# Feed-forward down projections by seven block products, and weight sums made by adding transfers in memory from launch on

## The chip, the cores and the metric

The kernel runs on one core of a Trainium2 chip. The metric is device time in microseconds (us), the median of several runs. A core has TensorE (PE, matrix products into the eight banks of PSUM), VectorE (DVE), ScalarE (ACT), GpSimd (POOL) and SyncE (SP), each with an instruction stream of its own, and 16 DMA engines that carry the transfers which SP, ACT and POOL issue. Engines wait for each other by semaphores.

## The reference

Two layers of a hybrid encoder work on 640 rows (512 of a prompt, 8 x 16 of samples) of 1024 features, in float32. Of each layer only the end matters here:

```python
def finish_layer(x, a, b, ga, gb, w_a, w_b, w_o, g1, b1, w_up, w_down, g2, b2):
    mix = (ga * (a @ w_a) + gb * (b @ w_b)) @ w_o
    x = layer_norm(ALPHA * x + mix, g1, b1)
    h = jnp.square(jax.nn.relu(x @ w_up)) @ w_down
    return layer_norm(ALPHA * x + h, g2, b2)
```

`w_up` is 1024 x 4096 and `w_down` 4096 x 1024. Before it stand one input projection, a differential attention of eight heads (against a cache of 512 positions) and a sliding-window attention.

## The kernel before

**Products.** Each float32 operand is split into a high part (`w_hi`, `xt_hi`, `act_a[0]`) and the rest (`w_lo`, `xt_lo`, `act_a[1]`), and each product is three matmuls: high x high, high x low, low x high. ACT makes the high part of a weight chunk (`high`, line 1245, or by halves `part_highs`, line 1753), DVE subtracts it for the low part (`low`, line 2133, or `part_low`, line 2755).

**Weights.** SP loads `weights` chunk by chunk (128 partitions x 1024, 512 KB, line 557) into a ring of four slots `w_raw`, in the order of use. A slot is free again when its low part is made. Weights arrive well ahead of TensorE as a rule.

**Feed-forward stage.** It runs in four parts of 1024 hidden features. The up projection of a part takes its output tiles in pairs: four pairs (in part 0 two plain tile pairs, then two such pairs). A pair (`combined_pair`) is a 2 x 2 block product with seven products in place of eight: the blocks are the halves of the contraction and of the 640 rows. For it DVE makes four sums of weight blocks per pair (`weight_sums`, lines 2734 to 2745) in the slots of `w_raw`, and the sums of the activations (`t`) are made once per layer. A pair is 7 x 4 x 3 = 84 matmuls of 320 columns. ACT copies PSUM banks to seed further sums (`up_seed`, line 1784), applies relu (lines 1799, 1806) and squares (lines 1893, 1898), and DVE makes the low part of the square (line 2783).

The down projection of a part is two calls of `row_group` (line 719 and the two after it): output halves of 512 columns, eight contraction tiles and five tiles of 128 rows, 2 x 8 x 5 x 3 = 240 matmuls of 512 columns, without blocks. DVE adds each finished bank into `rows` (line 2592). Order of work: up part 0, down part 0, up part 1, down part 1 and so on, the same in both layers.

**Launch.** The first products (line 1070) start when the first pieces of `x_t` and of two weight chunks are in; SP issues the rest of `x_t` behind them (lines 557 to 569). `x_t` is used one contraction tile after another, twelve matmuls for each.

**Heads.** For each of the eight heads ACT issues two loads of old keys (`kc`, 1 MB each, line 1304) and one of old values (`vc`, 2 MB, line 1312), each as soon as the previous head is through with the buffer. POOL has no work at all after the constants.

The diff touches the functions of the feed-forward stage on PE (`combined_pair`, `row_group` and the loop over parts), ACT and DVE, SP's order of loads, POOL's program, and many semaphore names, which are merged to free numbers.

## Time and profile before

| | us |
|---|---|
| median of 3 runs | 2148.25 (2148.22 to 2148.42) |
| the profiled execution, first to last instruction | 2145.2 |
| around the span (median less span) | 3.05 |
| PE busy | 2134.6 |
| DVE busy | 1469.7 |
| ACT busy | 1182.0 |
| POOL busy | 0.2 |

A view by stages (the windows view) gives for a stretch of time what each engine was busy and with how many instructions, the granted clock of TensorE (1.00 is its upper level, 2.4 GHz) and how busy the 16 DMA engines were. A group of instructions by line gives their mean duration. Matmuls overlap, so that their mean duration is not the time from one to the next. The timeline gives each instruction's start, and in brackets how long its engine had been idle before it and for whom.

### The profile page before, as it was taken

What the parts mean: (1) busy time and instruction counts of PE and PEld (TensorE: products, weight loads), DVE (VectorE), ACT (ScalarE), POOL (GpSimd) and SP (SyncE); (2) the same over time, 40 slices, a digit from 0 to 9 for tenths busy, and PEclk for the clock granted to TensorE, in tenths of its full rate; (3) what the DMA queues carried; (4) which work ended last, traced back from release to release, by engine and by line L of the source; (5) the groups of instructions that cost most, each with busy time, mean ns of one, the idle gap of its engine ahead of it and who ended that gap; (6) DMA issues with size and microseconds to landing.
All of it is one profiled execution on the core that took longest, in us unless ns stands there. A gap on an engine that the chain in (4) does not pass through costs nothing.

```text
span 2145.2 us, 38346 instructions
## 1 busy us (share of the span) xinstructions
PE 2134.6 (100%) x15100; PEld 1950.9 (91%) x15100; DVE 1469.7 (69%) x2420; ACT 1182.0 (55%) x2513; POOL 0.2 (0%) x4
## 2 busy tenths in 40 slices
PE   9999999999999999999999999999999999999998
PEld 7998889999989898989889888899999898989897
DVE  6757778677879373636667577786769793646466
ACT  4457776686625362627234677766865262627261
POOL 0000000000000000000000000000000000000000
PEclk9999999999999999999999999999999999999999
DMA  5367562421341222212333765525113412212231
GB/s 190 103 250 256 210 235 89 160 98 51 108 162 41 98 86 72 89 69 89 108 110 103 276 249 202 203 93 179 60 60 108 152 60 79 89 69 91 78 108 69
DMA packets 68162, 268.19 MB, mean 125 GB/s; under 512 B 10984, under 2 KB 12648, under 8 KB 61296
## 3 DMA queue, kind: packets, MB, share of 16 engines
q1 hardware_dynamic: 43136, 152.75, 20.2%
q10 hardware_dynamic: 24848, 112.99, 14.8%
q8 instruction: 121, 1.98, 0.4%
q14 instruction: 57, 0.47, 0.1%
HBM read 236.35 MB, written 25.95 MB: 122 GB/s over the span
## 4 chain that ended last, share of the span: by engine, by line
PE 98%; ACT 1%; DVE 0%; DMA 0%; issue 0%; DVEq 0%; ACTq 0%
PE PS L719 10%; PE PS L721 10%; PE PS L720 10%; PE PS L649 9%; PE PS L651 9%; PE PS L650 9%; PE PS L617 9%; PE PS L619 9%; PE PS L618 9%; PE PS L847 2%; PE PS L872 2%; PE PS L810 1%; PE PS L760 1%; PE PS L861 1%; PE PS L792 1%; PE PS L990 1%
## 5 line engine op out<-in xcount | busy, mean ns | idle before, releaser
L2133 DVE TENSOR_TENSOR w_lo<-w_raw,w_hi 128x1024 fp32r<-128x1024 f32 x178 | 215.9, 1222 | 243.9 <-ACT w_hi L1245 235.1
L617 PE MATMUL PS<-xt_hi,w_hi 128*128 128x320 f32 x1184 | 382.2, 323 | 0.3
L619 PE MATMUL PS<-xt_hi,w_lo 128*128 128x320 f32 x1184 | 365.7, 309 | 0.0
L618 PE MATMUL PS<-xt_lo,w_hi 128*128 128x320 f32 x1184 | 365.4, 309 | 0.0
L1245 ACT ACTIVATE w_hi<-w_raw 128x1024 fp32r<-128x1024 f32 x178 | 186.6, 1058 | 303.9 <-PE PS L721 284.2
L719 PE MATMUL PS<-w_hi,act_a_hi 128*128 128x512 f32 x800 | 312.3, 390 | 0.0
L720 PE MATMUL PS<-w_lo,act_a_hi 128*128 128x512 f32 x800 | 311.4, 389 | 0.0
L721 PE MATMUL PS<-w_hi,act_a_lo 128*128 128x512 f32 x800 | 311.4, 389 | 0.0
L617 PEld LDWEIGHTS PS<-xt_hi,w_hi 128*128 128x128 f32 x1184 | 222.7, 188 | 5.6 <-issue 4.3
L618 PEld LDWEIGHTS PS<-xt_lo,w_hi 128*128 128x128 f32 x1184 | 223.0, 188 | 0.1
L619 PEld LDWEIGHTS PS<-xt_hi,w_lo 128*128 128x128 f32 x1184 | 222.3, 188 | 0.0
L1272 ACT ACTIVATE rope_s<-PS 32x320 f32<-32x320 f32 x352 | 150.7, 428 | 56.1 <-DVE z_all L2124 28.2
L721 PEld LDWEIGHTS PS<-w_hi,act_a_lo 128*128 128x128 f32 x800 | 150.2, 188 | 31.5
L719 PEld LDWEIGHTS PS<-w_hi,act_a_hi 128*128 128x128 f32 x800 | 150.2, 188 | 31.4 <-issue 0.5
L720 PEld LDWEIGHTS PS<-w_lo,act_a_hi 128*128 128x128 f32 x800 | 150.2, 188 | 30.4
L2755 DVE TENSOR_TENSOR part_lo<-w_raw,part_hi 128x512 fp32r<-128x512 f32 x144 | 98.0, 688 | 56.2 <-ACT part_hi L1753 54.0
L1753 ACT ACTIVATE w_hi<-w_raw 128x512 fp32r<-128x512 f32 x130 | 78.5, 623 | 61.5 <-PE PS L721 48.8
L1753 ACT ACTIVATE part_hi<-w_raw 128x512 fp32r<-128x512 f32 x144 | 88.3, 623 | 31.1 <-DVE w_raw L2741 29.1
L649 PE MATMUL PS<-t_hi,part_hi 128*128 128x320 f32 x328 | 101.4, 309 | 0.0
L650 PE MATMUL PS<-t_lo,part_hi 128*128 128x320 f32 x328 | 101.4, 309 | 0.0
L651 PE MATMUL PS<-t_hi,part_lo 128*128 128x320 f32 x328 | 101.4, 309 | 0.0
L1784 ACT ACTIVATE PS<-PS 128x320 f32<-128x320 f32 x144 | 60.9, 423 | 69.7 <-PE PS L651 69.5
(338 smaller groups left out, 4770.6 us busy)
## 6 DMA issues: line engine op xcount, KB each, us to landing
w_raw<-in_weights SPq DMA_DIRECT2D x274, 512.0 KB, 3.5
kc<-in_k_cache ACTq DMA_DIRECT2D x32, 1024.0 KB, 7.9
vc<-in_v_cache ACTq DMA_DIRECT2D x16, 2048.0 KB, 8.7
gates_kept<-a_t ACTq DMA_DIRECT2D x8, 640.0 KB, 6.9
k_out<-k_t ACTq DMA_DIRECT2D x16, 320.0 KB, 2.4
v_out<-rows ACTq DMA_DIRECT2D x2, 2560.0 KB, 16.8
mix_a<-a_t ACTq DMA_DIRECT2D x2, 2560.0 KB, 12.2
rope_c<-gates_kept ACTq DMA_DIRECT2D x10, 320.0 KB, 3.1
```

Source lines behind the costliest of these rows:

```text
L617: mm(out, wh, hi[:, k, c], start=(k == 0), stop=False)
L618: mm(out, wh, lo[:, k, c], start=False, stop=False)
L619: last = mm(out, wl, hi[:, k, c], start=False, stop=(k == KT - 1))
L649: mm(up_bank(x), wh, moving[0][:, k], start=first and k == 0, stop=False, skip_group_check=True)
L650: mm(up_bank(x), wh, moving[1][:, k], start=False, stop=False, skip_group_check=True)
L651: last = mm(up_bank(x), wl, moving[0][:, k], start=False, stop=(k == KH - 1), skip_group_check=True)
L719: mm(out, xh, wh, start=(k == 0), stop=False)
L720: mm(out, xh, wl, start=False, stop=False)
L721: last = mm(out, xl, wh, start=False, stop=(k == KT - 1))
L1245: fn(w_hi[slot][:], raw[:, j, :], ACT.Copy).then_inc(w_hi_made[s], 1)
L1753: fn(parts_of(part)[0][part_place(n, o)][:], part_source(part, n, o), ACT.Copy) .then_inc(part_hi_made if o < 5 else w_hi_made[o - 5], 1)
L2133: v.tensor_tensor(w_lo[slot][:], raw[:, raw_of(s, n)[0], :], w_hi[slot][:].bitcast(F32), ALU.subtract)\
```

## The change

The diff has 1565 lines; these parts carry it.

1. The down projections of parts 1 and 2 (`BLOCK_PARTS`), in both layers, become block products too (`block_down`). The row tiles 0 and 2 against 1 and 3, the even against the odd contraction tiles, and the two output halves make 2 x 2 blocks: seven products of two row tiles each. Row tile 4 is computed in the plain way alongside. The 2 x 4 contraction steps are cut into eight "operands", each a weight block or a sum of blocks, of 1 to 3 output banks. Parts 0 and 3 keep `row_group`.
2. The sums of the weight blocks, those for the up pairs and those for `block_down`, are made in memory. POOL issues, from launch on and in one queue, 12 jobs of 8 transfers each (4 copies, 4 adding transfers, each waited for by the next that reads it). The transfers are 1 MB each, and 0.5 MB in the two jobs of part 0. DVE's `weight_sums` remain for the gates and the branches only.
3. A chunk of the feed-forward stage is now a slot of a second ring (`load_ring`, `ring_high`, `ring_low`): an up pair has four chunks (seven blocks of 512 columns), a `block_down` sixteen of 1024. SP waits for the job's sums before the first chunk of each part.
4. Around a `block_down`, DVE makes sums of the squared activations (`act_sums`), ACT and DVE split them (`sum_high`, `sum_low`), ACT copies pairs of banks (`block_seed`), and DVE adds banks into `rows` (`block_take`).

```diff
+BLOCK_PARTS = (1, 2)
+PAIR_RING, BLOCK_RING = 4, 16
+RING_SLOTS = 4
+TAKES = 9
+JOB_TRANSFERS = 8
...
+        RING = (8, 7, 0, 1)
...
+                else:
+                    if n in sums_at:
+                        sp.wait_ge(sum_dma, 16 * JOB_TRANSFERS * (sums_at[n] + 1))
+                    load_ring(n, j)
...
+        @block.gpsimd
+        def _(pool):
...
+            def put(dst, src):
+                pool.dma_start(dst, src).then_inc(sum_dma, 16)
+
+            def add(dst, src):
+                pool.dma_start(dst, src, accum_op=ALU.add, max_dma_last_dim=8 * D).then_inc(sum_dma, 16)
...
+                put(s1, a21)
+                put(s3, a11)
+                pool.wait_ge(sum_dma, 16 * (before + 2))
+                add(s1, a22)
+                add(s3, a21)
+                pool.wait_ge(sum_dma, 16 * (before + 4))
+                put(s2, s1)
+                pool.wait_ge(sum_dma, 16 * (before + 5))
+                add(s2, a11)
+                pool.wait_ge(sum_dma, 16 * (before + 6))
+                put(s4, s2)
+                pool.wait_ge(sum_dma, 16 * (before + 7))
+                add(s4, a12)
+                pool.wait_ge(sum_dma, 16 * (before + 8))
...
+            for j, (l, kind, part) in enumerate(SUM_JOBS):
+                (up_sums_of if kind == "up" else down_sums_of)(l, part, JOB_TRANSFERS * j)
...
+                operand(0, [(2, tile(0, 0), lambda: pe.wait_ge(d_taken, TAKES * d)),
+                            (3, tile(0, 2), lambda: pe.wait_ge(up_taken, 2 * q + 1)),
+                            (4, tile(0, 4), lambda: pe.wait_ge(c11_taken, q + 1))], True, even_ready)
+                operand(1, [(6, sum_tile(1, 0), lambda: pe.wait_ge(p5_copied, q + 1)),
+                            (7, sum_tile(1, 1), lambda: pe.wait_ge(up_taken, 2 * q + 2))], True,
+                        lambda u: u % 2 == 0 and pe.wait_ge(s_lo_ready, 5 * d + 1 + u // 2))
+                operand(2, [(0, sum_tile(2, 0), seeds(1)), (1, sum_tile(2, 1), None)], False,
+                        lambda u: u == 0 and pe.wait_ge(s_lo_ready, 5 * d + 3))
+                operand(3, [(2, tile(1, 0), None), (3, tile(1, 2), None), (4, tile(1, 4), None)], False, odd_ready)
+                operand(4, [(0, sum_tile(3, 0), seeds(2)), (1, sum_tile(3, 1), None)], False,
+                        lambda u: u == 0 and pe.wait_ge(s_lo_ready, 5 * d + 4))
+                operand(5, [(5, tile(0, 4), lambda: pe.wait_ge(c21_taken, q + 1))], True, lambda u: None)
+                operand(6, [(6, sum_tile(4, 0), None), (7, sum_tile(4, 1), None), (5, tile(1, 4), None)], False,
+                        lambda u: u == 0 and pe.wait_ge(s_lo_ready, 5 * d + 5))
+                operand(7, [(2, tile(1, 1), seeds(3)), (3, tile(1, 3), None)], False, lambda u: None)
...
-                        row_group(nth(l, AT_FF) + 8 * part + 4 + 2 * v, l * GROUPS + 4 + 2 * part + v,
-                                  act_a[0], act_a[1],
+                    if part in BLOCK_PARTS:
+                        block_down(l, part)
```

**POOL at launch.** POOL's stream before ended with the constants; this is what stands after them now, the first job (`up_sums` of layer 0, part 0) and the first row of the second:

```order
L759 DMA up_sums<-in_up_blocks 16x8192 x2
L762 DMA up_sums<-in_up_blocks 64x2048 [waits sum_dma]
L762 DMA up_sums<-in_up_blocks 64x2048
L759 DMA up_sums<-up_sums 16x8192 [waits sum_dma]
L762 DMA up_sums<-in_up_blocks 64x2048 [waits sum_dma]
L759 DMA up_sums<-up_sums 16x8192 [waits sum_dma]
L762 DMA up_sums<-in_up_blocks 64x2048 [waits sum_dma]
L759 DMA up_sums<-in_up_blocks 16x16384 [waits sum_dma]
```

Line 759 is a copy, line 762 an adding transfer; nothing but the queue's own semaphore holds them back.

**ACT at the start of the down projection of part 1.** The last rows of the up pair and what follows, in the kernel after; `w_hi_71`, `_69`, `_55`, `_56` are the four ring slots:

```order
L2267 ACTIVATE act_a_hi<-rope_s 128x640 [waits c21_taken,relu_odd]
L2272 ACTIVATE rope_s<-rope_s 128x640 [waits pair_hi_made]
L2321 ACTIVATE act_a_hi<-act_a_full 128x2x2x128 [waits s_sums] x2
L1589 ACTIVATE w_hi_71<-w_raw 128x1024 [waits ring_done,raw_loaded2]
L2330 ACTIVATE PS<-PS 128x1024 [waits d_taken,ring_done]
L2321 ACTIVATE s_hi<-s_full 128x1024 [waits s_sums]
L1589 ACTIVATE w_hi_69<-w_raw 128x1024 [waits ring_done,raw_loaded3]
L1589 ACTIVATE w_hi_55<-w_raw 128x1024 [waits ring_done,raw_loaded0]
L1589 ACTIVATE w_hi_56<-w_raw 128x1024 [waits ring_done,raw_loaded1]
L2321 ACTIVATE s_hi<-s_full 128x1024 [waits ring_done,s_sums]
```

Between the splits of weight chunks (line 1589) now stand splits of activation sums (line 2321) and copies of two banks (line 2330).

**DVE at the same place**, in the kernel after:

```order
L3225 SCALAR_TENSOR_TENSOR xt_full<-s_full,rope_s 128x256 [waits s_sums]
L3232 TENSOR_TENSOR act_a_lo<-act_a_full,act_a_hi 128x2x2x128 [waits s_hi_made] x2
L2541 TENSOR_TENSOR w_lo_72<-w_raw,w_hi_71 128x1024 [waits ring_hi]
L3232 TENSOR_TENSOR s_lo<-s_full,s_hi 128x1024 [waits s_hi_made]
L2541 TENSOR_TENSOR w_lo_70<-w_raw,w_hi_69 128x1024 [waits ring_hi]
L3250 TENSOR_TENSOR rows<-rows,PS 128x2x512 [waits row_evacuated0,ring_done,d_taken,row_evacuated1,row_evacuated2,row_evacuated3,row_evacuated4]
L3250 TENSOR_TENSOR rows<-rows,PS 128x2x512 [waits ring_done]
L2541 TENSOR_TENSOR w_lo_57<-w_raw,w_hi_55 128x1024 [waits ring_hi]
```

The low parts of the next chunks stand behind two additions into `rows` (line 3250), which wait for the end of operand 1.

## Rows read from the trace of the kernel before

**Rows 1.** The page: busy time by engine, and the granted clock in 40 slices:
```profile
PE 2134.6 (100%) x15100; PEld 1950.9 (91%) x15100; DVE 1469.7 (69%) x2420; ACT 1182.0 (55%) x2513; POOL 0.2 (0%) x4
...
PEclk9999999999999999999999999999999999999999
```
**Rows 2.** Waits of PE, all of them: line, waited for, us, times, longest:
```profile
PE PS L1078 <- DVE mask_cols L2904: 1.5, 1, 1.5
PE PS L1070 <- DVE xt_lo L2917: 0.9, 1, 0.9
```
**Rows 3.** Windows: down 0, up 1, down 1 of layer 0, down 2 of layer 1:
```profile
704.10:758.50 54.40, 54.40 (x242) 45.04 (x241) 21.91 (x27) 12.97 (x17) 0.00 (x0) 1.00 0.21 73
758.50:807.80 49.30, 49.30 (x338) 49.28 (x337) 33.59 (x52) 34.40 (x68) 0.00 (x0) 1.00 0.28 97
807.80:862.20 54.40, 54.40 (x242) 45.04 (x241) 21.91 (x27) 12.98 (x17) 0.00 (x0) 1.00 0.19 68
...
1979.10:2033.50 54.40, 54.40 (x242) 45.06 (x241) 21.88 (x27) 13.01 (x17) 0.00 (x0) 1.00 0.19 68
```
**Rows 4.** Groups by line and shape, 807.8 to 862.2: count, busy us, mean ns:
```profile
L720 PE MATMUL PS<-w_lo,act_a_hi 128*128 128x512 f32 x80 | 31.1, 389 | 0.0
...
L2133 DVE TENSOR_TENSOR w_lo<-w_raw,w_hi 128x1024 fp32r<-128x1024 f32 x7 | 8.6, 1225 | 26.8 <-ACT w_hi L1245 26.8
L1245 ACT ACTIVATE w_hi<-w_raw 128x1024 fp32r<-128x1024 f32 x7 | 7.4, 1059 | 32.0 <-PE PS L721 32.0
L2592 DVE SCALAR_TENSOR_TENSOR rows<-rows,PS 128x512 f32<-128x512 f32 x9 | 6.1, 687 | 4.1 <-PE PS L721 4.1
```
**Rows 5.** Groups by line and shape, whole span: a read of two banks, a narrow sum:
```profile
L1290 ACT ACTIVATE xt_hi<-PS 128x1024 fp32r<-128x1024 f32 x12 | 12.3, 1023 | 17.1 <-PE PS L1029 17.1
...
L2777 DVE TENSOR_TENSOR rope_c<-PS,p 128x320 f32<-128x320 f32 x28 | 13.6, 487 | 6.4 <-PE PS L651 6.2
```
**Rows 6.** Timeline of DVE after 807.8: start, duration, idle before and for whom:
```profile
811.57 0.82 DVE L2783 TENSOR_TENSOR act_a_lo<-rope_s,act_a_hi 128x640 fp32r<-128x640 f32 x1 [0.17 <-ACT rope_s L1898]
```
**Rows 7.** Windows: launch, before the first head, the first head's loads, the heads:
```profile
0.00:14.00 14.00, 11.53 (x62) 8.95 (x63) 8.15 (x15) 8.99 (x16) 0.20 (x4) 1.00 0.88 319
53.60:115.00 61.40, 61.40 (x369) 57.75 (x368) 44.79 (x63) 29.62 (x52) 0.00 (x0) 1.00 0.30 102
114.00:128.00 14.00, 14.00 (x98) 13.55 (x100) 4.73 (x6) 6.53 (x11) 0.00 (x0) 1.00 0.91 341
127.00:345.00 218.00, 217.87 (x2153) 189.28 (x2152) 161.69 (x388) 157.41 (x402) 0.00 (x0) 1.00 0.60 220
```
**Rows 8.** Timelines at launch, of ACT, of DVE and of PE:
```profile
11.48 1.37 ACT L1968 ACTIVATE xt_hi<-x_t 128x640 fp32r<-128x640 f32 x2 [1.02 <-DMA x_t<-in_x_cols]
...
12.25 3.22 DVE L2922 TENSOR_TENSOR xt_lo<-x_t,xt_hi 128x640 fp32r<-128x640 f32 x4 [0.95 <-ACT xt_hi L1968]
...
13.04 0.31 PE L1072 MATMUL PS<-xt_hi,w_lo 128*128 128x320 f32 x1
13.19 0.36 PE L1070 MATMUL PS<-xt_hi,w_hi 128*128 128x320 f32 x1
```
**Rows 9.** Transfers issued from 313 to 324, memory to memory: size, us to landing:
```profile
swk_keep_out<-in_swa_k_keep SPq DMA_DIRECT2D x1, 896.0 KB, 8.3
swv_keep_out<-in_swa_v_keep SPq DMA_DIRECT2D x1, 896.0 KB, 9.6
```
**Rows 10.** Window around those two copies:
```profile
313.00:324.00 11.00, 11.00 (x85) 9.41 (x85) 7.49 (x17) 6.55 (x17) 0.00 (x0) 1.00 0.90 367
```
**Rows 11.** The first head's second load of keys: issue, landing of both, first use:
```profile
117.14 0.36 ACTq L1304 DMA_DIRECT2D kc<-in_k_cache  x1
...
DMA to landing us min/median/max: 5.0/6.6/8.1
...
L760 PE MATMUL PS<-kc,z_all x256: 592/592/617, 127.6 to 1388.9; 128*32 128x512 f32 x128
```
**Rows 12.** DMA issues of the page, the slowest small load at launch:
```profile
cos<-in_cos_t SPq DMA_DIRECT2D x1, 320.0 KB, 8.1
```

More of the change, by code:

```diff
@@ L1925, in combined_pair @@
-                if u > first:
                     up_square(l, part, u - 1, 1)
-                if not begun and not second:
-                    up_fifth(l, part, u)
-                if not last:
-                    part_highs(l, part, u + 1, (1,))
-                else:
-                    high(0, down, skipped=1)
-                if not begun and not second:
-                    up_seed(l, part, u, 1)
-                if not last and not begun:
-                    part_highs(l, part, u + 1, (2,))
+                if not begun:
+                    ff_fifth(l, part, u)
@@ new lines, in block_down, with lows, takes @@
+            def block_down(l, part):
+                g = ring_block(l, part)
+                def lows(first, end):
+                    for c in range(first, end):
+                        ring_low(g + c)
+                def takes(*which):
+                    for i in which:
+                        block_take(l, part, i)
+                sum_low(l, part, 0)
+                sum_low(l, part, 1)
+                lows(4, 5)
+                sum_low(l, part, 2)
+                lows(5, 6)
+                takes(0, 1)
+                lows(6, 8)
+                sum_low(l, part, 3)
+                lows(8, 11)
+                sum_low(l, part, 4)
+                takes(2, 3)
+                lows(11, 13)
+                lows(13, 14)
+                takes(4)
+                lows(14, 17)
+                takes(5, 6)
+                lows(17, 19)
+                takes(7, 8)
+                lows(19, 20)
@@ L2871, in combined_pair @@
                     up_low(l, part, u, 0)
-                    low(1, down)
+                    next_low(l, part, u, 3)
                     up_low(l, part, u, 1)
+                    if block:
+                        act_sums(l, part, u)
             def constants():
```

771 lines of the change are left out of this document (544 added, 227 removed).

## The prediction

> **What bounds the kernel now.** The page comes first: PE is busy for 2134.6 of 2145.2 us, DVE for 69 and ACT for 55 per cent [rows 1]. The view of PE's waits is nearly empty, with 2.4 us, both at launch [rows 2]. So every microsecond of matmuls taken away is one of the span, as long as the other engines and the loads keep their lead; and everything that is late at TensorE is lost in full. The granted clock is at the 2.4 GHz level in every slice, so no part of the time hangs on it [rows 1]. The windows then show what a down projection costs: 54.4 us with PE busy throughout, the same in all parts and in both layers [rows 3]. In it are 3 x 80 matmuls [rows 4]; their mean duration of 389 ns overlaps with the next one's, for 240 x 0.389 would be 93 us. What one is worth is 54.4 / 240 = 0.2267 us. The 242 matmuls in the window's row include two at its edges.
>
> **The change, part by part.** The sum is made against the profiled span of 2145.2 us. The median lies 3.05 us above it, and that is added at the end.
>
> Matmuls. Counting `block_down`: its eight operands have 3, 2, 2, 3, 2, 1, 3 and 2 output banks, 18 in all, each with 4 steps of 3 matmuls: 216 of 512 columns in place of 240. It is 24 x 0.2267 = 5.44 us less, and with two parts in two layers 4 x 5.44 = **21.8 us** less. The up pairs keep their 84 matmuls.
>
> Work of ACT and DVE in a block projection, which now lasts 49.0 us. ACT splits 16 chunks at 1.06 us [rows 4], copies two banks three times at 1.02 us, the nearest row for that width [rows 5], and splits the activation sums (two of 512 and three of 1024 columns, 4.4 us): 24.5 us. DVE has 16 low parts at 1.225 us (19.6), the low parts of the sums (5.1), and nine additions into `rows`, five of them 1024 wide at 1.23 us and four at 0.69 [rows 4], 8.9 us: 33.6 us. Both fit into 49 us; before it was 13 and 22 [rows 3]. In the up pairs DVE sheds four weight sums each, and ACT splits three chunks of 1024 and a half one in place of seven halves, so that ACT's 34.4 of 49.3 us [rows 3] do not grow. All that is work beside PE and costs nothing.
>
> Hand-overs in a block projection. Counted from its start, the operands end at 8.2, 13.6, 19.0, 27.2, 32.6, 35.4, 43.5 and 49.0 us. The tightest is the first. Operand 1 needs the low part of the first activation sum at 8.2. Before, DVE ended the last low part of the squares at 811.57 + 0.82 = 812.4, which is 4.6 us after the projection's start [rows 6]. Four sums of 256 columns follow, at most 0.49 us each by the nearest row [rows 5], and one split of 0.69: 7.2 us, a lead of 1.0 us. The next is chunk 6. Its low part stands on DVE behind two additions into `rows` that wait for the end of operand 1 at 13.6; with 2 x 1.23 and 1.23 us it is made at 17.3, and operand 3 wants it at 19.0. In the second half the leads are 3 us and more, but for the sum of operand 6, 26.9 against 35.4. At the way back into the up pairs the first product of the next part is ready, and the bank copy it needs at 52.5 is done at 51.2. I put **0** for all this, with bounds of 0 and 1 us at each of three places in four projections, 12 us. As each lead is computed from durations that hardly vary, I take the low end, and 0.5 us for what I haven't seen.
>
> Launch. Here the new queue meets the busiest stretch. The engines are at 0.88 in the first 14 us [rows 7], and PE lives from hand to mouth: ACT waits for `x_t` 4 and 5 until 11.48, DVE makes the low part of 4 by 13.05, and PE takes it at 13.19, a beat late [rows 8]. Each microsecond that these loads lose is PE's. POOL now issues two copies of 0.5 MB right away and then two adding transfers of 0.5 MB. The two copies of 0.9 MB at 313 took, with two weight chunks and others, 4.04 MB in 11 us at 0.90 [rows 10], 2.45 us of all engines per MB; so 1.05 MB costs 2.6 us. The adding transfers begin when the copies have landed, at about 9 to 11 us, and take a share until `x_t` 6 and 7 are in; I put 1.4 us for that. Sum **4.0 us**, with bounds of 0 (the copies start too late and yield) and 8 (both adding transfers, twice a copy's cost, go before the last of `x_t`: 2.6 + 5.2). The Trainium skill (DMA: Bandwidth & Descriptors, Issuing engines are not separate DMA queues) says that transfers issued from GpSimd run on the same 16 engines as the others and interleave. No row of this trace shows a transfer from POOL beside SP's; if POOL's had engines of their own, the term would be 0 and the sum 4 us lower.
>
> The first head. Its second load of keys is issued at 117.1 and lands after 8.1 at most, at 125.2; PE wants the keys from 127.6 on, the second half of them a microsecond later [rows 11]. The engines are at 0.91 around it [rows 7]. If the queue takes a third of them, landing takes 12 us and PE waits 0.7 us; with half of them 16 us and 4.7. I take **1.5 us**, bounds 0 and 5. In the later heads a buffer is asked for some 22 us ahead and lands within 10, and the engines are at 0.60 [rows 7], so a doubled landing still fits. In layer 1 the queue should be done by its first head.
>
> The queue itself. SP waits for a part's sums before it loads them. A job is six transfers one after another (two of these steps with two at once). A copy of 896 KB landed in 8.3 us, and the second, with the first in flight, in 9.6 [rows 9]; that is 9.5 us for 1024 KB alone and 11 us for two at once. So the copies of a job take 11 + 9.5 + 9.5 = 30 us. No row shows an adding transfer. Its low bound is a copy's time, 30 us for a job's four; its high one the slowest landing per byte of the page, 8.1 us for 320 KB [rows 12], 26 us for 1024 KB, 104 us for four. A job is between 60 and 134 us. I take twice a copy, because an addition reads two sources and the copies are the nearest row: 30 + 60 = 90 us. Layer 0 has 5.5 such jobs (part 0's is half), due before the up projection of part 3, which began at 704.1 + 3 x 54.4 + 2 x 49.3 = 965.9 [rows 3]; less the 10.9 us saved by then and some lead for SP's loads, at about 950 us. 5.5 x 90 = 495 us: hidden, up to 950 / 5.5 = 173 us a job. The Trainium skill (Collectives: The Full Stack, The bandwidth ceiling) says that a reduction runs at about half a copy's rate, for its two source reads; a job would be 90 us by it, and nothing here shows it.
>
> Sum: 2145.2 - 21.8 + 4.0 + 1.5 + 0.5 = 2129.4 us of span, with 3.05 around it **2132.5 us**, 0.7 per cent less.
>
> **The rivals.**
>
> *Slower: the queue is late.* If a 1 MB job takes longer than 173 us (adding transfers of (173 - 30) / 4 = 36 us each, nearly four times a copy), SP stands at the sums of layer 0's part 3, all loads behind it in its queue stand too, and PE with them. Each microsecond above costs 5.5. It crosses zero at 176 us; at 200 us the loss is 5.5 x 27 = 149 in layer 0 and the time about 2280. For it: adding transfers are unknown here, six steps are in series, the heads' loads take 0.60 of the engines [rows 7], and POOL has never had work here. Against: even the high bound of 134 us leaves a lead of 950 - 5.5 x 134 = 213 us. The Trainium skill (SBUF — State Buffer, SBUF: two separate sides) has a rule that would bring it about: GpSimd cannot write a transfer's descriptors while VectorE runs an operation in a two-port mode. DVE is busy for 0.69 of the span [rows 1], and if POOL could issue in the rest only, the six steps of a job would be held up by some operations of 1 us each, 6 to 12 us a job, far from the 83 that are missing; so the chance of this rival is not raised by it.
>
> *No change: the leads are eaten.* Every hand-over of the blocks that misses costs PE. If the three places of a projection miss by 1.5 us each on top of their leads, it loses 4.5 of its 5.4 us, four of them 18 us, and the time is 2132.5 + 18 = 2150. For it: ACT and DVE serve three chains in one order there (chunks, activation sums, banks), and one that is late makes the others late. Against: the leads counted above, and engines for the loads that are 0.19 busy before [rows 3]. Contention alone would have to cost 17 us more than I count, over twice what the two high bounds (8 and 5) leave.
>
> *Much faster: the matmuls are worth their duration.* 96 x 0.389 = 37 us would give 2117. Only the mean duration speaks for it [rows 4], the windows speak against it [rows 3].
>
> **How the numbers follow.** The forecast (2126 to 2143.9) has 0.77. The queue that is late has 0.10, all of it slower. The eaten leads have 0.10, of which 0.09 lie within 0.2 per cent of 2148.25 (2143.95 to 2152.55, about what a measurement of this kernel can tell from no change) and 0.01 above. The price by duration and the like have 0.03. So faster 0.80, same 0.09, slower 0.11. The low end is 2126.0: the full 21.8 us with no loss at all is 2126.5. The high end is 2143.5: launch 8, head 5, and 2 of hand-overs give 2138.5, and 5 us are put on for several missed leads. Outside lie some 0.2.
>
> **What would show it.** PE should have 15100 - 96 = 15004 matmuls, a block projection should last 49.0 us with PE busy throughout, and PE's waits should stay empty but for launch and the first head. The first product with `x_t` 4 should start at about 17 us, not 13.2. POOL's transfers of a job should take 60 to 135 us in all and end for layer 0 by 740. Wrong would be: a wait of SP for the sums, PE idle between operands, or loads of keys that land after 12 us in later heads too.

## The result and the profile after

The changed kernel takes **2186.32 us** (median of 4 runs, 2183.24 to 2193.83) against 2148.32 beside it on the same chip: a ratio of **1.0183**, with an interval of 1.0165 to 1.0201. The prediction was 2132.5 with a range of 2126.0 to 2143.5. It is wrong in size and in sign, by 54 us. The profiled execution took 2187.98 us, its span 2186.2. (In one run further down, **e3_no_queue**, one of ten executions went at a granted clock of 0.654 and took 2981.4 us; the ratio there leaves it out.)

The page's busy row answers to [rows 1]. PE has 96 matmuls fewer, as counted, and yet stands at 97 per cent instead of 100:

```profile
PE 2129.3 (97%) x15004; PEld 1939.3 (89%) x15004; DVE 1469.5 (67%) x2336; ACT 1232.6 (56%) x2493; POOL 65.4 (3%) x100
```
The page's row of the clock still has a 9 in every slice; a slice is 55 us wide. The windows further down show what that hides.

The view of PE's waits, two rows before [rows 2], now has twelve, of which the eight costliest stand here (line, waited for, us, times, longest):

```profile
PE PS L911 <- ACT PS L2154: 15.5, 20, 0.9
PE PS L822 <- ACT rope_s L1622: 9.3, 1, 9.3
PE PS L1394 <- DVE xt_lo L3405: 7.0, 3, 4.8
PE PS L1116 <- ACT a_t L1729: 3.2, 1, 3.2
PE PS L1084 <- DMA kc<-in_k_cache: 2.9, 2, 1.5
PE PS L1043 <- DVE rows L3000: 2.6, 1, 2.6
PE PS L1043 <- DVE w_lo L2534: 2.5, 1, 2.5
PE PS L981 <- issue: 1.6, 4, 0.4
```
They fall into two kinds. The first row is 20 short waits in the up pairs, ten in each layer and hardly different from each other, which points to the program's own order. All others but the small issue gaps are single events of 1 to 9 us: at launch, at the first keys, at the gates, and in the output projection. Together the twelve are 48.9 us.

Windows show what stands beside them (length, PE, PEld, DVE, ACT, POOL busy, granted clock, DMA share, GB/s): at launch, behind the first keys, and around the wait at 461:

```profile
20.00:30.00 10.00, 8.81 (x45) 8.81 (x46) 8.00 (x15) 4.74 (x8) 1.22 (x1) 0.70 1.04 401
...
140.00:150.00 10.00, 8.68 (x75) 6.13 (x68) 2.47 (x5) 4.41 (x11) 0.00 (x0) 0.83 1.04 341
...
450.00:460.00 10.00, 1.55 (x13) 1.30 (x12) 0.00 (x0) 4.09 (x8) 0.52 (x1) 0.80 1.13 262
460.00:470.00 10.00, 9.14 (x46) 9.18 (x47) 4.70 (x9) 6.62 (x13) 0.37 (x1) 0.69 0.95 387
```
The DMA engines are full in each of them, where launch was at 0.88 and the heads at 0.60 before [rows 7]; and the granted clock falls behind PE's longer waits, to 0.69 from 460 to 470. So a wait costs more than its own length: around 461 PE waits for 1.2 and 9.3 us and loses 13.4. Its timeline has the longer wait, and products of 0.47 us behind it that take 0.31 at the clock's upper level. Eighteen of them start 0.27 us apart in place of 0.147:

```profile
460.86 0.61 PE L822 MATMUL PS<-xt_hi,w_hi 128*128 128x320 f32 x1 [9.31 <-ACT rope_s L1622]
461.26 0.47 PE L823 MATMUL PS<-xt_lo,w_hi 128*128 128x320 f32 x1
```

If the matmuls of both kernels are put side by side by their order, the lag of the changed kernel reads: +10.2 us at 30, +14.9 after the first head, +19.6 before the gates, +33.5 behind them, +39.9 at the feed-forward stage of layer 0, and +41.0 at the end. In this sum are 20.5 us that the block projections gave back (5.1 each, below). So 61 us were lost, against 6 in the prediction. (The median of the kernel before, run again beside the experiments, was between 2147.28 and 2148.40, so that medians of different runs can be compared to about 1 us.)

### The profile page after: what moved, and what is told of

Same layout as the page of the kernel before. It is cut to its first block, busy times and chain, and to the rows that moved or that the text cites. A ratio compares the mean times of both kernels' runs of the same rounds, so it can differ in the third digit from the quotient of the medians.

```text
span 2186.2 us, 38210 instructions
## 1 busy us (share of the span) xinstructions
PE 2129.3 (97%) x15004; PEld 1939.3 (89%) x15004; DVE 1469.5 (67%) x2336; ACT 1232.6 (56%) x2493; POOL 65.4 (3%) x100
## 3 DMA queue, kind: packets, MB, share of 16 engines
q0 software_dynamic: 7936, 92.28, 16.5%
## 4 chain that ended last, share of the span: by engine, by line
PE 86%; ACT 5%; issue 3%; DMA 3%; DVE 2%; SPq 0%; ACTq 0%; DVEq 0%
PE PS L822 9%; PE PS L824 8%; PE PS L823 8%; PE PS L1043 6%; PE PS L1045 6%; PE PS L1044 6%; PE PS L855 3%; PE PS L856 3%; PE PS L857 3%; PE PS L911 3%; PE PS L913 3%; PE PS L912 3%; PE PS L981 3%; PE PS L982 3%; PE PS L983 3%
## 5 line engine op out<-in xcount | busy, mean ns | idle before, releaser
L824 PE MATMUL PS<-xt_hi,w_lo 128*128 128x320 f32 x1184 | 367.2, 310 | 0.0
L823 PE MATMUL PS<-xt_lo,w_hi 128*128 128x320 f32 x1184 | 367.1, 310 | 0.0
L2541 DVE TENSOR_TENSOR w_lo<-w_raw,w_hi 128x1024 fp32r<-128x1024 f32 (+1 forms) x176 | 199.3, 1138 | 125.3 <-ACT w_hi L1589 125.0
L1589 ACT ACTIVATE w_hi<-w_raw 128x1024 fp32r<-128x1024 f32 (+1 forms) x176 | 172.3, 985 | 83.9 <-PE PS L983 64.1
L1043 PE MATMUL PS<-w_hi,act_a_hi 128*128 128x512 f32 x480 | 187.9, 391 | 5.1 <-DVE rows L3000 2.6
L1045 PE MATMUL PS<-w_hi,act_a_lo 128*128 128x512 f32 x480 | 186.9, 389 | 0.0
L1044 PE MATMUL PS<-w_lo,act_a_hi 128*128 128x512 f32 x480 | 186.9, 389 | 0.0
L911 PE MATMUL PS<-t_hi,w_hi 128*128 128x320 f32 x448 | 139.9, 312 | 15.5 <-ACT PS L2154 15.5
L912 PE MATMUL PS<-t_lo,w_hi 128*128 128x320 f32 x448 | 138.4, 309 | 0.0
L913 PE MATMUL PS<-t_hi,w_lo 128*128 128x320 f32 x448 | 138.4, 309 | 0.0
L913 PE MATMUL PS<-xt_hi,w_lo 128*128 128x320 f32 x336 | 103.8, 309 | 0.0
L912 PE MATMUL PS<-xt_lo,w_hi 128*128 128x320 f32 x336 | 103.8, 309 | 0.0
```

The source lines that it names most:

```text
L823: mm(out, wh, lo[:, k, c], start=False, stop=False)
L824: last = mm(out, wl, hi[:, k, c], start=False, stop=(k == KT - 1))
L911: mm(up_bank(x), wh, moving[0][:, k], start=first and k == 0, stop=False, skip_group_check=True)
L912: mm(up_bank(x), wh, moving[1][:, k], start=False, stop=False, skip_group_check=True)
L913: last = mm(up_bank(x), wl, moving[0][:, k], start=False, stop=(k == KH - 1), skip_group_check=True)
L1043: mm(out, xh, wh, start=(k == 0), stop=False)
```

## Two causes, and the experiments that part them

**Theory A.** Two independent losses. (1) The hand-written order of DVE in the up pairs is late for the copy that seeds a bank; 20 waits. (2) POOL's queue costs time wherever a load with a short lead runs beside it (`x_t` at launch, the first keys, issues on ACT's queue, the row loads), and none elsewhere. **Rival B.** The queue costs by its bytes, wherever it runs: the DMA engines are a shared resource, and 92 MB more cost about 37 us. Under B no placement helps.

### The order in the up pairs

DVE, ACT and PE around the end of such a pair, in the changed kernel (start, duration, instruction, idle before and for whom):

```profile
810.28 1.23 DVE L2541 TENSOR_TENSOR w_lo<-w_raw,w_hi 128x1024 fp32r<-128x1024 f32 x1 [1.63 <-ACT w_hi L1589]
811.42 0.48 DVE L3201 TENSOR_TENSOR rope_c<-PS,p 128x320 f32<-128x320 f32 x1
...
811.94 0.47 ACT L2169 ACTIVATE rope_c<-rope_c 128x320 f32<-128x320 f32 x1 [1.69 <-DVE rope_c L3201]
...
814.48 0.43 ACT L2154 ACTIVATE PS<-PS 128x320 f32<-128x320 f32 x1
...
815.05 0.39 PE L911 MATMUL PS<-t_hi,w_hi 128*128 128x320 f32 x1 [0.69 <-ACT PS L2154]
```
DVE idles 1.63 us for a weight's high part, which ACT ends at 810.25, makes its low part (810.28), and only then does the addition (811.42), for which ACT is idle 1.69 us. Everything after it on ACT is late by that 1.7 us, the seed at 814.48 included, and PE waits 0.69. From one product's start to the next the twenty places cost 0.85 or 1.06 us each, 18.7 in all, more than the idle time in the rows of waits. The seed before the same product in the kernel before, and in the kernel with the exchange that follows:

```profile
773.50 0.43 ACT L1784 ACTIVATE PS<-PS 128x320 f32<-128x320 f32 x1
...
774.36 0.31 PE L649 MATMUL PS<-t_hi,part_hi 128*128 128x320 f32 x1
```
```profile
821.14 0.43 ACT L2154 ACTIVATE PS<-PS 128x320 f32<-128x320 f32 x1
```
The kernel before had DVE's low part before the addition too, but for half a chunk (0.69 us, behind ACT's split of 0.61), and the seed ended 0.43 us before its product. With the exchange it ends 1.1 us before it (the product starts at 822.66). Nothing needs the low part first. **e1_swap** exchanges the two instructions:

```diff
                 ff_add(l, part, u, 1)
-                next_low(l, part, u, 2)
                 ff_add(l, part, u, 0)
+                next_low(l, part, u, 2)
```


> The changed kernel with one edit: in an up pair DVE makes the second addition (ff_add of the even tile) before the low part of the next chunk, not after it. Theory A: the 20 waits of PE for ACT's bank copy (15.5 us, 0.69 to 0.90 each, with the restart 0.92 to 1.13) come from that order alone, since the low part (1.23 us) stands between the end of the pair's sixth product and ACT's relu. They vanish, and the time is 2186.3 - 20 = 2166 us. Rival B: ACT's queue is simply full in an up pair (its work grew), or the transfers slow the ring; then the waits stay and the time is 2186 within 3.

Measured: 2163.88 us (2161.63 to 2174.67, before 2147.28; ratio 1.0085, interval 1.0059 to 1.0111). The row for line 2154 is gone from PE's waits; those that remain are single events, of which the two longest are:

```profile
PE PS L822 <- ACT rope_s L1622: 11.2, 1, 11.2
PE PS L1043 <- DVE w_lo L2534: 9.4, 1, 9.4
```
Two instructions in another order are worth 22 us (2186.3 to 2163.9, as expected), of a loss that no line of the prediction mentions.

### The queue taken away

**e3_no_queue** has DVE's old order and no transfer from POOL. The loads of sums are loads of the plain blocks of the same size, so it computes other products; what SP loads and what PE, ACT and DVE do is the same.

```diff
-                        src = (up_blocks if kind[0] == "a" else up_sums)[l, b, p]
+                        src = up_blocks[l, b, p]
...
-            for j, (l, kind, part) in enumerate(SUM_JOBS):
-                (up_sums_of if kind == "up" else down_sums_of)(l, part, JOB_TRANSFERS * j)
```


> The changed kernel without POOL's transfers and SP's waits for them; where a sum was loaded, a block of the weights is loaded in its place (so this kernel computes other products, the same number of bytes in the ring and the same matmuls). Theory A: it is the floor for moving the queue, 2186.3 - 39.4 = 2147 us, and the 20 waits for ACT's bank copies stay at 15 us. Rival B: if the queue also slows the feed-forward stage, it falls further, to 2125 us, and the waits go with it.

Measured: 2149.65 us (2148.81 to 2150.63 in nine of ten executions), ratio 1.0010 (1.0000 to 1.0019). All of PE's waits of this kernel:

```profile
PE PS L907 <- ACT PS L2150: 15.4, 20, 0.9
PE PS L977 <- issue: 1.6, 4, 0.4
PE PS L1398 <- DVE mask_cols L3383: 1.5, 1, 1.5
PE PS L1390 <- DVE xt_lo L3396: 0.9, 1, 0.9
```
The 20 waits for the seed are there without the queue and have the same length; every single event is gone. So the queue costs 2186.3 - 2149.7 = 36.7 us, and the order, whose waits are untouched by it, some 20. It doesn't yet tell A from B: both say 37 us for the whole queue.

### A window that looked quiet

**e2_window** (old order) and **e4_both** (exchange too) hold the whole queue until the first item of the sliding attention, so that launch and heads are free of it.

```diff
+            pool.wait_ge(swa_scores, 1)
             for j, (l, kind, part) in enumerate(SUM_JOBS):
```


> The changed kernel, but POOL waits with its first job until the first scores of the window attention of layer 0 (about 430 us from the start). Theory A: the 39 us that the trace of after has lost before the feed-forward stage of layer 0 are contention of the queue with the loads of launch, heads and gates. All of it goes: 2186.3 - 39 = 2147 us, and the stage at launch is as in the kernel before. The queue of 11 units of 54 us then ends at about 1040, and the sums are in time. Rival B: the same transfers cost the same wherever they run, since the engines are shared: 2175 us or more. Rival C: the queue is now late, SP stands at the sums, and the time is above 2186.

> Both edits: DVE's addition before the low part, and the queue begun at the window attention. Theory A: the two causes add up, 2186.3 - 39 - 20 = 2127 us, which is the kernel before less the 21.8 us of matmuls. Rival B: with one cause gone the other takes its place, 2140 us or more.

Measured: 2190.60 us (2184.39 to 2195.42; ratio 1.0198, 1.0174 to 1.0222) and 2169.63 (2159.44 to 2174.42; 1.0110, 1.0092 to 1.0127). Both expectations missed, by 43 us each. The queue ran from 439 to about 1100 us, launch and heads were clean, and the loss was as large as before; it had moved. The two costliest of PE's waits of e4_both:

```profile
PE PS L1044 <- DVE w_lo L2535: 13.5, 1, 13.5
PE PS L912 <- ACT PS L2155: 8.9, 4, 4.1
```
By themselves these two runs speak for rival B. What they show when read closer is where a lead is short in that stretch as well. The 13.5 us: DVE stands at `rows`, whose load takes twice its time. The DMA view of 585 to 625 shows it, first in the kernel before, then in e4_both (queue, packets, MB, share of the engines; then an issue, its KB and the time to landing):

```profile
q1 hardware_dynamic: 1717, 6.25, 45.7%
...
rows<-in_x_rows ACTq DMA_DIRECT2D x1, 2560.0 KB, 12.0
```
```profile
q0 software_dynamic: 457, 5.71, 53.6%
q10 hardware_dynamic: 944, 3.67, 23.9%
q1 hardware_dynamic: 719, 2.65, 16.8%
...
rows<-in_x_rows ACTq DMA_DIRECT2D x1, 2560.0 KB, 25.5
```
POOL's queue (q0), with at most two transfers in flight, holds 53.6 per cent of the engines' time; SP's (q1) falls from 45.7 to 16.8, and the load of `rows` takes 25.5 us in place of 12.0. DVE's timeline has the consequence:

```profile
618.39 2.36 DVE L2535 TENSOR_TENSOR w_lo<-w_raw,w_hi 128x1024 fp32r<-128x1024 f32 x2 [17.85 <-DMA rows<-in_x_rows]
```
In the feed-forward stage it is the ring: before the 4.1 us wait at 1021.5 ACT had stood 4.73 us for a load of sums (line 1590, at 1017.27), and these loads of 256 KB landed in 12.6 us there. The view of SP's waits has none for the sums themselves, so the queue was not late.

### Only the launch, or only until the first head

**e6_after_launch** holds the first job until the launch's chunks are in use (22 us), **e7_first_head** until PE has the second step of the first head's keys (130 us); all else follows without a pause, with the exchange in both.

```diff
+            paced = {
+                    0: lambda: pool.wait_ge(chunk_done[1], 1),
+            }
             for j, (l, kind, part) in enumerate(SUM_JOBS):
+                if j in paced:
+                    paced[j]()
```
In e7_first_head the wait is `pool.wait_ge(dec_scores, 2)`.

> The exchange of two DVE instructions, and the first job held until the launch's last chunk is in use (about 20 us); nothing else of the queue is changed. Theory A: the launch no longer loses its 10 us and the later losses of the queue stay: 2154. Rival B (by bytes): the queue's cost stays, 2164. The launch's waits of PE should fall from about 8 us to the 2.4 us of the kernel before.

> The exchange of two DVE instructions, and the first job held until PE is in the second step of the first head's keys (about 130 us); the later jobs follow without a pause. Theory A: launch (10 us) and the first keys (4 us) are free; but the queue now stands about 110 us later, so that the head loads around 312, ACT's issue at 446, and perhaps the row loads around 600 meet it: 2150 to 2160. By the theory that an earlier begin is what costs, 2150. Rival B: 2164.

Measured: 2164.82 us (2148.04 to 2172.09; ratio 1.0072, 1.0051 to 1.0092) and 2159.18 (2156.20 to 2170.31; 1.0060, 1.0039 to 1.0082). e7 is where it was expected. e6 is not: the launch's waits did fall, to 3.2 us against 2.4 before, but its median is that of e1_swap, not 10 us less. A queue that runs without a pause is a chain of 72 steps; begun 20 us later it is later everywhere, and meets other loads. e6's single executions are 24 us apart. The profiled one, its fastest, lost 5.6 us for `w_lo` in the output projection and 4.3 in the gates. So these two runs tell how little a later begin is worth by itself: at most 5 us in the median. That they met other loads further on is read from their profiles and not tested apart.

### Copies in place of additions

**e8_copies** makes the adding transfers plain copies of the same size (so the sums, and the results, are other ones), with the exchange:

```diff
-                pool.dma_start(dst, src, accum_op=ALU.add, max_dma_last_dim=8 * D).then_inc(sum_dma, 16)
+                pool.dma_start(dst, src, max_dma_last_dim=8 * D).then_inc(sum_dma, 16)
```


> The exchange of two DVE instructions, and the queue's adding transfers made plain copies of the same size (so the sums are other ones: part of the computation is changed). If the adding transfers are what is heavy (two sources read, twice a copy's work), a job falls from 54 us in quiet stages to about 40, and the queue's loss of some 37 us falls to about 25: 2152. If each transfer loads the engines by the bytes it writes only, whatever it does with them, the loss and the time of the exchange alone remain: 2164, and a job takes 54 us.

Measured: 2148.69 us (2145.73 to 2158.00; ratio 1.0009, 0.9996 to 1.0021): 15 us less than e1_swap, 21 more than the best kernel below. It is the fall that was expected of heavy additions, and a little more. The pages' rows of the queue, of the changed kernel and of e8_copies (packets, MB, share of 16 engines' span):

```profile
q0 software_dynamic: 7936, 92.28, 16.5%
```
```profile
q0 software_dynamic: 7936, 92.28, 11.5%
```
With as many packets and bytes, 0.165 x 2186.2 = 361 us of all engines against 0.115 x 2150.8 = 247. A copy is 247 / 92.28 = 2.68 us per MB, and the half that adds then (361 - 124) / 46.14 = 5.1: an adding transfer takes 1.9 times a copy's engine time. A whole job in the quiet stretch before the heads, from its first issue to the next job's, took 53.9 us in the changed kernel (44.41 to 98.32), and 44.2 in e8_copies (39.57 to 83.77).

### The queue in pieces

Rival B falls only if the same 92 MB, moved in the same kernel, can cost nothing. **e5_paced** cuts the queue at jobs; **e9_finer** at single transfers, so that it also rests for the first keys of each layer. Both have the exchange. The gates of e9_finer, as (job, transfer):

```diff
+            gates = {
+                    (0, 0): lambda: pool.wait_ge(chunk_done[1], 1),
+                    (1, 7): lambda: pool.wait_ge(dec_scores, 2),
+                    (3, 0): lambda: pool.wait_ge(swa_scores, 1),
+                    (5, 6): lambda: pool.wait_ge(h_ready, 8),
+                    (6, 0): lambda: pool.wait_ge(x_lo_ready, tiles_before(1, 0) + ROW_STEPS),
+                    (7, 7): lambda: pool.wait_ge(dec_scores, 2 * HEADS + 2),
+                    (9, 0): lambda: pool.wait_ge(swa_scores, ITEMS + 1),
+                    (11, 6): lambda: pool.wait_ge(h_ready, 32 + 8),
+            }
```
The queue runs from 22 to about 105 us, 132 to 219, 440 to 592, 710 to 725, and in layer 1 from 1073 to 1165, 1190 to 1277, 1498 to 1648 and 1768 to 1782.

> The exchange of two DVE instructions as before, and POOL's queue cut into five pieces that begin where the loads have a lead: jobs 0 and 1 when the last product of the launch group has begun (about 20 us), 2 and 3 after the keys of the first head (about 132), 4 to 6 after the first item of the sliding attention (about 430), 7 and 8 in layer 1 (about 1085), 9 and 10 after its first keys (1210), 11 at its sliding attention (1510). Theory A (the queue costs time only where a load with a short lead runs beside it: launch, first keys, the issues on ACT's queue around 312 and 446, the row loads around 600): all of these but the last are avoided, and what is left is the saving of 21.8 us and some 2 to 7 us of leftovers: 2127 to 2133. Rival B (the queue costs by its bytes, wherever it runs, about 37 us for 12 jobs): as with the exchange alone, 2164.

> The exchange of two DVE instructions, and the queue in pieces as in the run before, but cut finer: it now also rests during the first keys of either layer and in the later heads, and does that work in the sliding attention and at the first down projection instead. Theory A (the queue costs where a load has a short lead): of the 13 us that the profile of the coarser pacing lost, the 1.3 and 2.9 us of waits for keys and the 2.8 and 2.3 us of ACT's held issue go, with the clock's share: 2128 to 2132. Rival B (a cost by bytes, of which the coarse pacing hid a part by luck): 2139, as there.

Measured: e5_paced 2139.64 us (2135.88 to 2141.99; ratio 0.9959, 0.9944 to 0.9974), 6.6 above its expectation; **e9_finer 2127.66 us** (2127.31 to 2128.08, before 2148.22; ratio **0.9905**, 0.9891 to 0.9920), within it. That beats both kernels, and its runs are 0.8 us apart where the changed kernel's are 11. What e5_paced lost more stands at the head of its waits, 5.1 us for ACT's `a_t` and 4.9 for keys. These are all that e9_finer has:

```profile
PE PS L1422 <- DVE mask_cols L3407: 1.6, 1, 1.6
PE PS L1414 <- DVE xt_lo L3420: 0.8, 1, 0.8
```
These two rows are those of [rows 2] again. Every one of the 96 transfers is still made, as the page's row of the queue shows:

```profile
q0 software_dynamic: 7936, 92.28, 17.1%
```
So rival B falls: the bytes cost nothing if they are moved where the loads have a lead. That lead need not be a quick landing. In its pieces beside the heads (132 to 219 us) the DMA share was 1.01 and keys landed after up to 18.2 us, and PE never waited.

### The same kernel with one cause put back

**e10_old_order** is e9_finer with the exchange undone. **e11_launch_back** is e9_finer without its first gate, so that the queue begins at launch again.

> The finer pacing with DVE's old order of the two instructions, so with that one change undone. If the cost of the order (20 waits of PE for the seed, 15.4 us of waits and 1.6 of issue where no queue ran) is independent of the queue, this is 19 to 22 us slower than the finer pacing, about 2150. If the waits came in part from transfers beside them, it is under 10 us slower.

> The finer pacing with the queue begun at launch again: the first gate alone is taken away. Theory A: PE waits at launch as in the changed kernel, 8 us and some granted clock, so 7 to 10 us slower than the finer pacing, 2137 to 2141; jobs 0 and 1 end earlier, at about 100 us, which costs nothing. By the prediction's term for the launch it would be 4 us slower; by the rival (cost by bytes) nothing changes.

Measured: 2149.83 us (2148.63 to 2150.99; ratio 1.0008, 0.9998 to 1.0017) and 2134.12 (2132.69 to 2136.25; 0.9936, 0.9921 to 0.9951), so 22.2 and 6.5 us above e9_finer. The waits for the seed of e10_old_order, and the costlier row of the launch in e11_launch_back:

```profile
PE PS L931 <- ACT PS L2174: 15.4, 20, 0.9
```
```profile
PE PS L1413 <- DVE xt_lo L3424: 3.9, 2, 2.3
```
The order costs 22 us with a harmless queue and 2186.3 - 2163.9 = 22 with the greedy one, so the two causes are independent. Of the 22 us, 18.7 are lost at the twenty seeds and 2.2 at one place in each of the four block projections, as is shown further down. The first is just above what was expected. The second is half a microsecond under its 7 to 10, but more than the 4.0 of the prediction, and far from the zero of rival B.

The sum closes: e9_finer is 20.6 us under before; the order adds 22.2 (2149.8), and the queue without pauses 36.5 (2186.3).

### Why the queue wins against the loads

One thing was open: how two transfers in flight can hold half of the engines' time against the loads of SP and ACT. **e12_small** is e1_swap (the queue without a pause, from launch on) with every transfer of the queue in rows of 2 KB, where the additions had 8 and the copies 64:

```diff
-                return t.rearrange("u p n -> (u p n)").rearrange("(a n) -> a n", n=2 * D)
+                return t.rearrange("u p n -> (u p n)").rearrange("(a n) -> a n", n=D // 2)
...
-                pool.dma_start(dst, src).then_inc(sum_dma, 16)
+                pool.dma_start(dst, src, max_dma_last_dim=2 * D).then_inc(sum_dma, 16)
...
-                pool.dma_start(dst, src, accum_op=ALU.add, max_dma_last_dim=8 * D).then_inc(sum_dma, 16)
+                pool.dma_start(dst, src, accum_op=ALU.add, max_dma_last_dim=2 * D).then_inc(sum_dma, 16)
```


> The kernel with the exchange alone, its queue begun at launch and without a pause, but with every transfer of the queue in rows of 2 KB instead of 8 (additions) and 64 KB (copies): the same bytes, the same steps. In the page before this edit a packet of the queue held 92.28 MB / 7936 = 11.6 KB, one of SP's queue 2.8 KB. Theory P (the engines take turns between queues by packets, so that the larger packet wins the larger share): the queue's share beside other loads falls, a job takes longer than the 56 us it took in the quiet stretch, and the 36 us that the queue costs fall to 10 to 25: 2138 to 2153. Rival Q (the share doesn't depend on the packet's size): the time stays at 2164, or rises, as smaller rows take more engine time for the same bytes.

Measured: 2148.96 us (2142.05 to 2157.73; ratio 1.0005, 0.9992 to 1.0018), 15 us less than e1_swap. The queue's row of the page, which in e1_swap read 7936 packets and 16.6 per cent:

```profile
q0 software_dynamic: 35328, 92.28, 18.5%
```
The same bytes in 4.5 times as many packets, of 2.6 KB now, and with more engine time in all. But beside other loads its share falls; the DMA view of 100 to 160 us, e1_swap and then e12_small:

```profile
q0 software_dynamic: 547, 7.34, 43.1%
...
kc<-in_k_cache ACTq DMA_DIRECT2D x4, 1024.0 KB, 14.8
```
```profile
q0 software_dynamic: 1896, 5.29, 34.9%
...
kc<-in_k_cache ACTq DMA_DIRECT2D x4, 1024.0 KB, 11.1
```
The queue moves 5.29 MB there in place of 7.34, and the keys land in 11.1 us in place of 14.8. The first two jobs take 120 us, not 100. The load of `rows` shows it too: it lands in 15.2 us, against 21.4 in e1_swap and 25.5 in e4_both. So theory P is borne out and Q is not: the larger packets had won the queue a larger share. The Trainium skill (DMA: Bandwidth & Descriptors, Queues, rings and completion order) says that each engine takes its queues in turn by packets; the runs agree. It is a cure for less than half of the 36 us, and placement is one for all. With packets smaller than SP's (3.7 KB) and ACT's (5.5 KB) the queue still held 34.9 per cent there, and it still cost 21 us against e9_finer.

## Where the prediction failed, step by step

**Matmuls: right.** 15004 of them. A block projection from its first product to the next part's lasts 49.3 us in e9_finer, against 49.0 said and 54.4 before; the window of e9_finer around the first of them:

```profile
809.00:858.00 49.00, 49.00 (x216) 40.31 (x216) 34.37 (x35) 25.97 (x29) 0.00 (x0) 1.00 0.49 161
```
The four give 20.5 us, not 21.8. That a matmul is worth 0.2267 us and not its mean duration of 0.389 stands as well.

**ACT and DVE in a block projection: right as sums, and nearly as hand-overs.** 24.5 and 33.6 us were counted, 26.0 and 34.4 are measured. Of the hand-overs through chunks, activation sums and banks, which I worked out one by one, one missed: the one at operand 1, the tightest of the prediction. In each of the four projections PE stood for 0.4 us before that operand's first product; in the first projection:

```profile
859.17 0.47 PE L981 MATMUL PS<-w_hi,act_a_hi 128*128 128x512 f32 x1 [0.41 <-issue]
```
The low part of the first activation sum was ready 8.66 us after the projection's start and not 7.2, because the pair before had handed over its last squares late (their low part was done at 6.6 and not at 4.6). That is the late order of the pairs again. With the exchange (e9_finer) the squares are done at 4.8 and the sum's low part at 6.85, against the 8.2 when it is wanted, and there is no gap at all.

**The up pairs: the step that failed first.** "In the up pairs DVE sheds four weight sums each, and ACT splits three chunks of 1024 and a half one in place of seven halves, so that ACT's 34.4 of 49.3 us [rows 3] do not grow. All that is work beside PE and costs nothing." Both halves of the sentence are true (the four pairs of a part took ACT 34.2 us and DVE 29.6 in e9_finer, from 858.3 to 907.5, against 34.4 and 33.6 [rows 3]) and its conclusion is not. A sum of busy time says whether an engine can keep up over the pair, not whether one instruction is in time. I followed the order of DVE through the block projections, where it was new, and did not through the pairs, where the chunk had grown from 512 to 1024 columns: a split of 1.06 us on ACT and a low part of 1.23 on DVE now stood ahead of an addition with ACT and PE behind it, where the seed had had 0.43 us to spare. Price: 0, bounds 0; measured 22 us. It alone takes the whole gain.

**Launch: right mechanism, low price.** 4.0 us with bounds 0 and 8. Measured by itself 6.5, within the bounds. Single executions scatter: in the profile of the changed kernel the lag is 10.2 by 30 us and in that of e11_launch_back 6.8, against 1.6 in that of e9_finer. The place was right, and so was the order of events, but the queue's share was not: the product after the longest wait was said to start at about 17 us and starts at 21.2:

```profile
21.19 0.64 PE L1394 MATMUL PS<-xt_hi,w_hi 128*128 128x320 f32 x1 [4.83 <-DVE xt_lo L3405]
```
What the sum has no term for is the clock: 0.70 from 20 to 30 us, where 16 products behind the wait started 0.27 us apart in place of 0.147, 2 us in all.

**The first head: right mechanism, low price.** 1.5 us with bounds 0 and 5; by the lag it was 4.7 (10.2 to 14.9), of which 2.9 is waiting, and the rest falls with the clock of 0.83 behind it.

**The later heads: the step that failed second.** "In the later heads a buffer is asked for some 22 us ahead and lands within 10, and the engines are at 0.60 [rows 7], so a doubled landing still fits." The landing did fit, though it was later than the prediction's own sign of being wrong (after 12 us in later heads too): up to 20.4 us, and no wait of PE for it. The issue did not. From ACT's timeline in the changed kernel (`ACTq` is the issue of a transfer):

```profile
312.46 4.50 ACTq L1654 DMA_DIRECT2D kc<-in_k_cache  x1
...
317.55 1.75 ACT L1622 ACTIVATE rope_s<-PS 32x320 f32<-32x320 f32 x4 [4.49 <-issue]
```
```profile
446.40 9.37 ACTq L2424 DMA_DIRECT2D s_v<-in_swa_vc  x1
...
455.81 0.63 ACT L2428 ACTIVATE sk_dup<-sk_t 64x512 f32<-64x512 f32 x1 [6.89 <-issue]
```
The same two issues in the kernel before:

```profile
297.48 0.45 ACTq L1304 DMA_DIRECT2D kc<-in_k_cache  x1
...
422.78 1.38 ACTq L2024 DMA_DIRECT2D s_v<-in_swa_vc  x1
```
Issues that took 0.45 and 1.38 us hold ACT for 4.50 and 9.37, and ACT's arithmetic stands behind them. PE waits 3.2 and 9.3 us. The first is for the last head's keys, the second is the window attention's load behind the heads. I had treated the lead of the data as the only thing that contention can touch. Behind the longer hold POOL's queue held 93.2 per cent of the engines' time from 446 to 456. Full engines alone don't do it: in the kernel before they were at 0.94 from 182 to 190 us, and an issue of keys in that stretch took 0.64. Nor is it plain for the shorter one, for the share was 1.21 from 305 to 312 but 0.30 from 312 to 317. Why an issue is held stays open; in e9_finer, where none took more than 2.1 us, PE waits for none.

**What stands behind the heads: left out.** The prediction names launch and first head as the places where the queue meets a short lead, and leaves out the stretch at the gates (13 us lost at 446 to 470, by the second of the issues above) and the output projection (5 us). The search for short leads ended at the first two found.

**The queue's speed: wrong, in the other direction.** 90 us a job, with bounds of 60 and 134, was put against 54 in the quiet stretch and 73 to 82 in the heads; all twelve jobs were done by about 715 us. "Twice a copy" for an adding transfer was nearly right as engine time (1.9). In time to landing it was too much: in e5_paced's job from 499.5 to 554.5 us the three steps of copies took 8.9, 6.6 and 6.0 us, where 11, 9.5 and 9.5 were said, and the three of additions 15.1, 9.7 and 8.7, where 60 in all were said. The Trainium skill's half of a copy's rate for a reduction (Collectives: The Full Stack, The bandwidth ceiling) agrees with the engine time and not with the landing. The rival that was given most of the slower side, a queue that is late, did not occur: the queue was hundreds of microseconds early. That it was so early is what could have been asked about: layer 0 needed 5.5 jobs by 950 and had them at 392, layer 1's were not loaded before 1725, and all of them were moved in the first 715 us, through the busiest stages. I computed whether it would be in time and took the excess for safety.

**The chances.** "Contention alone would have to cost 17 us more than I count" was an argument by my own high bounds. It cost 36.5 us, 31 above the 5.5 of the sum. A slower result had 0.11, nearly all of it for the wrong mechanism. The sum of the high end is wrong too: the full saving with launch 8, head 5 and 2 of hand-overs is 2126.5 + 15 = 2141.5 and not 2138.5, so that with 5 us put on it would have been 2146.5. The result lies outside that as well.

## What to carry to other kernels

Background transfers are paid for by the load with the least lead that runs beside them, not by their bytes: list every load and every issue between the first and the last background transfer with its lead, and release the queue at events of the compute engines, in pieces, where that lead is long, and keep its packets as small as those of the loads. A greedy queue that is far ahead of its deadline is a warning, and a spread of 10 to 24 us between executions of an otherwise steady kernel went with it in these runs.

When an operand's size changes, follow the order of the engine that makes it instruction by instruction up to the next hand-over to TensorE, also where the totals fall.

## What the runs showed of the hardware

- A queue issued by POOL, never more than two transfers in flight, held 53.6 per cent of the DMA engines' time from 585 to 625 (e4_both, 12.5 KB a packet) while SP's queue, with 7 chunks to carry, had 16.8 and ACT's, with 3.7 MB, 23.9. The Trainium skill (DMA: Bandwidth & Descriptors, Issuing engines are not separate DMA queues) has it that such transfers share the 16 engines, and the trace agrees; that the shares are so unequal was the surprise.
- An adding transfer from memory to memory took 1.9 times a copy's engine time per byte. In the changed kernel 1 MB landed, in the median of 20 each, after 8.9 us against a copy's 7.0 one at a time, and after 13.9 against 7.9 two at once.
- The issue of a transfer on ACT's queue held ACT for up to 9.37 us (11.31 in e1_swap) where the same one took 1.38 before. POOL's queue held 93.2 per cent of the engines' time meanwhile. With the engines at 0.94 and no such queue (the kernel before, 182 to 190 us) an issue took 0.64.
- In the changed kernel the granted clock read 0.70 from 20 to 30 us, where PE's wait of 4.8 us ends, 0.83 at the two waits of 1.5 and 1.3 close together (140 to 150), 0.86 behind the one of 3.2 (320 to 330) and 0.69 behind the one of 9.3. Two single waits of 2.5 us (640 to 665) left it at 1.00, but 0.83 stood around one of 2.3 at the launch of e11_launch_back (15 to 25). Over the whole span it was 0.994, so the page's row of the clock does not show it.
- POOL could issue all through: its transfers of 1 MB took it 0.5 to 0.8 us each, with DVE busy for two thirds of the time, and no issue longer than 1.34 us.
